# Turned tiles first in their step, and a last half tile in quarters, in a fused attention and mLSTM block

## Chip, core and metric

One core of a Trainium2 chip (trn2) runs the whole block. The metric is the device time of one execution in microseconds, lower is better. "Low parts" below are the remainders of numbers split in two: every float32 matrix is used as a high part (rounded to the TensorE input format) and a low part (what the rounding lost), and a product of two matrices is made of three matmuls, high x high, high x low and low x high.

## What is computed

For 512 tokens of width 1024: an RMS norm, one projection to ten groups of columns, attention with 8 heads of 64 on rotated queries and keys, an mLSTM with 4 heads of 128, both normed and gated, one output projection, an RMS norm of it, and the residual. At this length all blocks are selected, so that attention is plain causal attention. The part that the change works on is the end of it:

```python
ya = rms_norm(attention(...), attn_out_g[l]) * jax.nn.silu(az)
ym = jax.nn.sigmoid(mo) * hm * jax.nn.silu(mz)
y = jnp.einsum('bsc,cd->bsd', jnp.concatenate([ya, ym], axis=-1), w_out[l])
x = x + rms_norm(y, post_norm_g[l])
```

## The kernel before

Tokens lie in 4 tiles of 128 partitions. Weights come in slots of 256 KB through a ring; ScalarE cuts the high part (`cut`, L708), VectorE or GpSimd the low part (L922, L591). A first stage runs slot by slot: projections, and beside them the mLSTM heads, with the keys and queries turned by TensorE (`turn_k`, L1539, and `turn_q`, L1549) and split by `kt_high` (ScalarE, L696) and `kt_low` (VectorE, L1132). `qk_low` (L1052) is the low part of the mLSTM's queries and keys, which `head_scores` needs.

The second stage is a list of steps, 0 to 39, written out by hand in `EVENTS`; each engine walks the same list in program order and meets the others at semaphores. Step s holds, for a unit of attention (one head of one query tile, 32 in all, tile 3 first):

- even s: TensorE makes the scores of units s and s+1 (`pair_scores`, L1646), into banks 6 and 7; VectorE masks them (L1256); ScalarE makes the exponential (`exp_of`, L854);
- TensorE transposes the probabilities of unit s-2 (L1696), ScalarE copies their high part (`pt_high`, L862), VectorE makes the low part (`pt_low`, L1262);
- TensorE multiplies unit s-3 with the values (`wide_values`, L1667, for tiles 3 to 1, `tile_values`, L1679, for tile 0). For odd s VectorE sums two finished units (`y2_sum`, L1247) out of bank 2. `wide_values` of an even unit waits for the sum of the two units before it, since it writes the same bank.

In between TensorE works at products of the projections and of the output (`z_part`, `om`, `oa`, L1355 to L1357), two to four in a step. In eight steps (9, 13, 17, 21, 23, 25, 31, 36; `TURNS`) a finished tile of ym or ya is turned so that it can be multiplied with the output weights: TensorE transposes it into bank 6 (`turn`, L1615), ScalarE copies it (`turn_high`, L801), VectorE makes the low part (`turn`, L1213). The next `pair_scores` waits for that, because bank 6 is the same one.

The output is made in halves of 512 columns for each of 4 tiles, as `(i, c)` with i = 0 to 3 and c = 0, 1; i = 3 is the first tile of tokens. The steps of a half are: four products (`oa`), the sum with the mLSTM's part (`y_sum`, L1292), its squares (ScalarE, L899), the product with the norm's gain (`y_gain` on GpSimd, L640; for i = 3 on VectorE, L1298); for each tile the mean (`y_mean`, L1302 and L1304), the reciprocal root (GpSimd, L556), the write (`y_out`, L1312) and the stores (`store`, all on the SP queue, L458).

Of the kernel before, what the change touches and what calls it, by code (L numbers as in the profile page):

```python
# [20 lines left out]
ALU = mybir.AluOpType  # L21
ACT = mybir.ActivationFunctionType

P = 128
# [67 lines left out]
for _h, _g in enumerate(("az", "ak", "av", "aq")):  # L92
# [18 lines left out]
N_WIDE = AH * (NT - 1)  # L111
EVENTS = {}

PRIORITY = ("mz", "mz_late", "z", "om_out", "cut", "slot", "z_part", "om", "oa", "q_T", "q_out", "ya_half", "y", "ya", "y_sq", "ya_sq",
            "ya_ms", "y_fin", "y_end", "turn")


def _event(step, kind, *what):
# [34 lines left out]
OA_ORDER = ((0, 0, 27), (1, 0, 28), (0, 1, 30), (1, 1, 33), (2, 0, 35), (2, 1, 36), (3, 0, 37), (3, 1, 38))  # L153
OA_OF = {(_i, _c): _n for _n, (_i, _c, _at) in enumerate(OA_ORDER)}
for _i, _c, _at in OA_ORDER:
    for _k in range(4):
        _event(_at, "oa", _i, 4 * _c + _k)
    _event(_at + int(_at < 35), "y", _i, _c)
    _event(_at + 1, "y_sq", _i, _c)
for _i, (_mean, _end) in enumerate(((33, 34), (35, 36), (37, 37), (39, 39))):  # L160
    _event(_mean, "y_fin", _i)
    _event(_end, "y_end", _i)
for _i in range(NT):
    _s = AH * _i + AH - 1 + LAG_PV
    _late = int(_i < NT - 1)
# [9 lines left out]
def _sharers():  # L175

    where, last, now = {}, {0: ("mz", 0), 1: ("mz", 1)}, 1
    starts = {"z_part": "z", "om": "om", "oa": "oa"}  # L180
    for s in range(STEPS):
        for kind, what in [e for e in EVENTS.get(s, ()) if e[0] in starts]:
            if what[-1] % (NK if kind == "z_part" else 4) == 0:
                user = (starts[kind], OA_OF[what[0], what[1] // 4] if kind == "oa" else what[0])
                if user == ("oa", OA_OF[NT - 1, 0]):
# [15 lines left out]
def build(nc, x, pre_g, w_in, i_bias, f_bias, conv_w, conv_b, attn_g, mlstm_g, w_out, post_g, rope, out):  # L201
    with ExitStack() as ctx:
# [57 lines left out]
        msa = sb("msa", [P, NT])  # L260
        ra = sb("ra", [P, NT])
        ssy = sb("ssy", [P, 2 * NT])
        msy = sb("msy", [P, NT])
        ry = sb("ry", [P, NT])

# [33 lines left out]
        ya = f_part(F_YA, 2, AW)  # L299
        yb = f_part(F_Y, 2, D)  # L300
        yg = tmp.rearrange("p a c -> p (a c)")
        kT_hi = r_part(R_KT, 4, SEQ)
        kT_lo = r_part(R_KT + 4 * SEQ, 4, SEQ)
        v_hl = r_part(R_V, NT * AH, 2 * DH)
# [115 lines left out]
        oa_ps = sem("oa_ps")  # L420
        y_done = sem("y_done")
        ssy_done = sem("ssy_done")
        msy_done = sem("msy_done")
        ry_done = sem("ry_done")
        y_gained = sem("y_gained")
# [35 lines left out]
        def _(sp):  # L461
# [45 lines left out]
            sp.wait_ge(out_done[0], 32)  # L507
            load_residual(3)
            store(sp, 2)
            store(sp, 3)  # L510
            for i in range(NT):
                sp.wait_ge(out_done[i], 32)


        @block.gpsimd
        def _(g):
# [118 lines left out]
            def y_gain(i, c):  # L635

                n = OA_OF[i, c]
                g.wait_ge(post_in, 16)
                g.wait_ge(ssy_done, n + 1)
                g.tensor_tensor(yb[:, i % 2, c * AW:(c + 1) * AW], yb[:, i % 2, c * AW:(c + 1) * AW],  # L640
                                post[:, c * AW:(c + 1) * AW], ALU.mult).then_inc(y_gained, 1)

            for s in range(STEPS):
                for kind, what in EVENTS.get(s, ()):
                    i = what[0]
                    if kind == "cut":
                        cut(i)
                    elif kind == "ya" and i < NT - 2:
                        ya_norm(i)
                    elif kind == "ya_ms":  # L650
                        g.wait_ge(msa_done, i + 1)
                        rsqrt(ra[:, i:i + 1], msa[:, i:i + 1]).then_inc(ra_done, 1)
                    elif kind == "y_sq" and i < NT - 1:
# [46 lines left out]
        def _(a):  # L700
# [163 lines left out]
            for s in range(STEPS):  # L864
                events = EVENTS.get(s, ())
                for kind, what in events:
                    if kind == "mz":
                        mz_evac(a, *what)
                    elif kind == "z":
                        z_evac(a, *what)  # L870
                    elif kind == "om_out":
                        om_evac(a, *what)
                    elif kind == "cut":
                        cut(*what)
                if LAG_T <= s < NU + LAG_T:
# [1 line left out]
                if s < NU:  # L877
                    exp_of(s)
                for kind, what in events:
                    if kind == "turn":  # L880
                        turn_high(*what)
                    elif kind == "mz_late":
                        mz_evac(a, *what)
                for kind, what in events:
                    i = what[0]
                    if kind == "q_out":
                        q_high(i)
                    elif kind == "ya_sq":
                        a.wait_ge(ya_done, i + 1)
                        junk_free()  # L890
                        squares["ya"] += 1
                        a.activation(gains[:], ya[:, i % 2, :], ACT.Square,
                                     accum_out=ssa[:, i:i + 1]).then_inc(ssa_done, 1)
                    elif kind == "y_sq":
                        i, c = what
                        a.wait_ge(y_done, OA_OF[i, c] + 1)
                        junk_free()
                        squares["y"] += 1
                        a.activation(gains[:], yb[:, i % 2, c * AW:(c + 1) * AW], ACT.Square,  # L899
                                     accum_out=ssy[:, 2 * i + c:2 * i + c + 1]).then_inc(ssy_done, 1)  # L900

        @block.vector
        def _(v):
# [255 lines left out]
            for b in range(S_QK, LAST_SLOT + 1):  # L1161
# [123 lines left out]
            def y_sum(i, c):  # L1285
# [4 lines left out]
                if i >= 2:  # L1290
                    v.wait_ge(out_ready, 2 * (i - 1))
                v.scalar_tensor_tensor(out=yb[:, i % 2, cols], in0=shared("oa", n)[:], scalar=ra[:, i:i + 1],  # L1292
                                       in1=y_mlstm[:, c, NT - 1 - i, :], op0=ALU.mult, op1=ALU.add).then_inc(y_done, 1)
                if i == NT - 1:
                    v.wait_ge(y_done, n + 1)
                    v.wait_ge(post_in, 16)
                    v.wait_ge(ym_gated, NT)
                    v.tensor_tensor(yg[:, cols], yb[:, i % 2, cols], post[:, cols], ALU.mult).then_inc(y_gained, 1)  # L1298

            def y_mean(i):  # L1300
# [5 lines left out]
            def y_out(i):  # L1306
                v.wait_ge(ry_done, i + 1)
                v.wait_ge(xr_in[i], 16)
                v.wait_ge(y_gained, OA_OF[i, 1] + 1)
                for c in range(2):  # L1310
                    cols = slice(c * AW, (c + 1) * AW)
# [4 lines left out]
            for s in range(STEPS):  # L1316
                events = EVENTS.get(s, ())
                if s < NU:
                    mask(s)
                if 0 <= s - LAG_FOLD < N_WIDE and s % 2 == 1:  # L1320
                    y2_sum(s - LAG_FOLD)
                for kind, what in events:
# [4 lines left out]
                if LAG_T <= s < NU + LAG_T:  # L1327
                    pt_low(s - LAG_T)
                for kind, what in events:
                    if kind == "turn":  # L1330
                        turn(*what)
                    elif kind == "mz_late":
                        mz_gate(*what)
                for kind, what in events:
                    if kind == "q_out":
# [6 lines left out]
                        ya_scale(*what)  # L1342
                    elif kind == "y":
                        y_sum(*what)
                    elif kind == "y_fin":
                        y_mean(*what)
                    elif kind == "y_end":
                        y_out(*what)
# [3 lines left out]
        def _(pe):  # L1352
# [265 lines left out]
            def oa(i, k):  # L1618
# [8 lines left out]
                if kk == 3:  # L1627
                    mm.then_inc(oa_ps, 1)

            def pair_scores(s):  # L1630

                t, h = unit(s)
# [50 lines left out]
            for s in range(STEPS):  # L1683
                events = EVENTS.get(s, ())
                if s < NU and s % 2 == 0:
                    pair_scores(s)
                u = s - LAG_T
                if 0 <= u < NU:
                    t, h = unit(u)
# [10 lines left out]
                    turn_y2(s - LAG_YT)  # L1700
                    turn_y2(s - LAG_YT + 1)
                for kind, what in events:
                    if kind == "turn":
                        turn(*what)
                for kind, what in events:
                    if kind == "slot":
                        mz_slot(*what)
                    elif kind == "q_T":
# [4 lines left out]
                        om_part(*what)  # L1713
                    elif kind == "oa":
                        oa(*what)
                u = s - LAG_PV
                if 0 <= u < NU:
                    pe.wait_ge(pt_lo, u + 1)
# [32 lines left out]
```

## Time and profile before

| | us |
|---|---|
| median of 3 runs | 335.34 (334.81 to 335.36) |
| profiled execution | 335.24 |
| its span | 333.5 |
| TensorE busy | 317.8 |
| VectorE busy | 227.5 |
| ScalarE busy | 172.2 |
| GpSimd busy | 99.9 |

The span is what the profiler records of the instructions; 1.7 us lie around it. Matmuls are pipelined, so that a single one of 512 columns is shown as 0.39 us long while the next one starts 0.23 us later: distances between starts say more than durations. The mean granted TensorE clock is 0.992 of full speed. The engines' steps run one behind the other within each engine, and an idle time in front of an instruction is put down to the semaphore that came last.

### The profile page before, as it was taken

How to read it: one execution, taken by the hardware profiler on the slowest of the kernel's cores; microseconds unless marked ns; L12 is line 12 of the kernel's file. 1: busy time of each engine (PE TensorE's matmuls, PEld its weight loads, DVE VectorE, ACT ScalarE, POOL GpSimd, SP SyncE). 2: the span in 40 equal slices, each digit the busy share in tenths (PEclk: the TensorE clock that was granted, in tenths of full speed). 3: DMA queues.
4: the chain of work that ended last, by engine and by line, in shares of the span. 5: the costliest groups of instructions: out<-in, count | busy, mean ns of one | idle time of the engine just before them, and what ended most of it. 6: DMA issues, size and time to landing. Idle time of an engine off the chain costs nothing.

```text
span 333.5 us, 5022 instructions
## 1 busy us (share of the span) xinstructions
PE 317.8 (95%) x1614; PEld 260.9 (78%) x1614; DVE 227.5 (68%) x530; ACT 172.2 (52%) x341; POOL 99.9 (30%) x121
## 2 busy tenths in 40 slices
PE   8999999999999999899999999999999998998790
PEld 5887788888888888688888888788888887887580
DVE  2544999678996589876995487575766743435785
ACT  3448653696373524845346522655548647354330
POOL 8001003207240240002400054880025724154451
PEclk9999999999999999999999999999999999999996
DMA  7931544842736552246425232200001401602044
GB/s 225 286 96 32 166 129 107 164 140 82 127 85 157 147 87 64 63 126 132 76 63 159 70 89 66 90 37 2 0 2 63 172 19 43 211 23 105 0 156 160
DMA packets 26873, 33.51 MB, mean 100 GB/s; under 512 B 3752, under 2 KB 15056, under 8 KB 26848
## 3 DMA queue, kind: packets, MB, share of 16 engines
q1 hardware_dynamic: 25712, 30.51, 30.6%
q0 software_dynamic: 1120, 2.68, 6.2%
q8 instruction: 13, 0.21, 0.3%
q14 instruction: 12, 0.10, 0.1%
q10 hardware_dynamic: 16, 0.00, 0.0%
HBM read 31.06 MB, written 2.13 MB: 100 GB/s over the span
## 4 chain that ended last, share of the span: by engine, by line
PE 84%; DVE 9%; issue 4%; ACT 2%; DVEq 0%; POOLq 0%; POOL 0%; ACTq 0%
PE bank L1355 21%; PE bank L1357 21%; PE bank L1356 21%; PE bank L1402 3%; PE bank L1646 3%; PE bank L1696 3%; PE bank L1667 2%; PE bank L1490 1%; PE bank L1383 1%; PE bank L1370 1%; DVE farena L1043 1%; DVE xT_lo L1213 1%; PE bank L1657 1%; ACT xT_hi L801 1%; DVE w_lo L922 1%
## 5 line engine op out<-in xcount | busy, mean ns | idle before, releaser
L1355 PE MATMUL bank<-w_hi,xT_hi 128*128 128x512 f32 x272 | 110.7, 407 | 0.0
L1357 PE MATMUL bank<-w_hi,xT_lo 128*128 128x512 f32 x272 | 106.7, 392 | 0.0
L1356 PE MATMUL bank<-w_lo,xT_hi 128*128 128x512 f32 x272 | 106.1, 390 | 0.0
L708 ACT ACTIVATE w_hi<-w_raw 128x512 fp32r<-128x512 f32 x88 | 53.2, 626 | 59.2 <-PE bank L1357 58.8
L1357 PEld LDWEIGHTS bank<-w_hi,xT_lo 128*128 128x128 f32 x272 | 51.0, 188 | 11.4
L1355 PEld LDWEIGHTS bank<-w_hi,xT_hi 128*128 128x128 f32 x272 | 51.2, 188 | 9.1 <-issue 0.4
L1356 PEld LDWEIGHTS bank<-w_lo,xT_hi 128*128 128x128 f32 x272 | 51.3, 189 | 8.8
L922 DVE TENSOR_TENSOR w_lo<-w_raw,w_hi 128x512 fp32r<-128x512 f32 x64 | 45.1, 719 | 5.0 <-ACT w_hi L708 4.5
L591 POOL TENSOR_TENSOR w_lo<-w_raw,w_hi 128x512 fp32r<-128x512 f32 x24 | 31.2, 1320 | 48.4 <-ACT w_hi L708 48.4
L862 ACT ACTIVATE rarena<-bank 128x512 fp32r<-128x512 f32 (+3 forms) x32 | 13.8, 435 | 26.0 <-PE bank L1696 26.0
L1256 DVE CUSTOM_DVE_ANT_0 farena<-bank,causal 128x512 f32<-128x512 f32 (+3 forms) x32 | 15.4, 483 | 17.1 <-PE bank L1646 17.1
L1355 PE MATMUL bank<-xT_hi,w_hi 128*128 128x512 f32 x64 | 25.7, 402 | 0.0
L1357 PE MATMUL bank<-xT_hi,w_lo 128*128 128x512 f32 x64 | 25.1, 393 | 0.0
L1356 PE MATMUL bank<-xT_lo,w_hi 128*128 128x512 f32 x64 | 25.0, 391 | 0.0
L1262 DVE TENSOR_TENSOR rarena<-bank,rarena 128x512 fp32r<-128x512 f32 (+3 forms) x32 | 15.6, 489 | 13.7 <-ACT rarena L862 13.5
L1043 DVE SCALAR_TENSOR_TENSOR farena<-farena,pcol 128x512 f32<-128x512 f32 x24 | 18.8, 783 | 0.8
L854 ACT ACTIVATE farena<-farena,mx 128x512 f32<-128x512 f32 (+3 forms) x32 | 17.8, 556 | 2.6 <-DVE mx L1256 2.5
L571 POOL DMA_DIRECT2D farena<-g_rows x16 | 8.6, 546 | 33.8 <-DVE farena L1063 32.2
L1063 DVE SCALAR_TENSOR_TENSOR farena<-bank,farena 128x512 f32<-128x512 f32 (+3 forms) x16 | 7.8, 488 | 14.4 <-PE bank L1357 14.4
L556 POOL TENSOR_TENSOR vr<-vs,mhalf 128x2 f32<-128x2 f32 x8 | 5.7, 709 | 37.5 <-DVE vs L1102 37.5
L1696 PE MATMUL bank<-ident,farena 128*128 128x128 f32 x80 | 14.9, 284 | 0.0
L1646 PE MATMUL bank<-rarena 64*128 64x512 f32 (+3 forms) x96 | 11.7, 347 | 3.2 <-DVE xT_lo L1213 1.9
(195 smaller groups left out, 522.8 us busy)
## 6 DMA issues: line engine op xcount, KB each, us to landing
w_raw<-in_w_in SPq DMA_DIRECT2D x72, 256.0 KB, 2.9
w_raw<-in_w_out SPq DMA_DIRECT2D x16, 256.0 KB, 2.7
farena<-in_x SPq DMA_DIRECT2D x4, 256.0 KB, 4.7
farena<-in_x SPq DMA_DIRECT2D x2, 512.0 KB, 7.5
farena<-g_rows POOLq DMA_DIRECT2D x4, 256.0 KB, 3.9
silu_az<-in_x SPq DMA_DIRECT2D x2, 512.0 KB, 3.7
w_raw<-in_x SPq DMA_DIRECT2D x2, 512.0 KB, 3.3
out_y<-silu_az SPq DMA_DIRECT2D x4, 256.0 KB, 2.0
```

What stands on the lines that cost most here:

```text
L591: g.tensor_tensor(w_lo[:, n % RING, :], w_raw[:, n % RAW, :], w_hi[:, n % RING, :].bitcast(F32), ALU.subtract).then_inc(w_lo_done[n % 2], 1)
L708: a.activation(w_hi[:, n % RING, :], w_raw[:, n % RAW, :], ACT.Copy).then_inc(w_hi_done, 1)
L854: a.activation(prob[:, s % 2, 0:n], sm[:, s % 2, 0:n], ACT.Exp, scale=-1.0, bias=mx[:, s:s + 1], accum_out=rsum[:, s:s + 1]).then_inc(prob ...
L922: v.tensor_tensor(w_lo[:, n % RING, :], w_raw[:, n % RAW, :], f32(w_hi[:, n % RING, :]), ALU.subtract).then_inc(w_lo_done[n % 2], 1)
L1043: ins = v.scalar_tensor_tensor(out=acc, in0=u[:, j:j + SEQ], scalar=tap[j], in1=acc, op0=ALU.mult, op1=ALU.add)
L1256: v.tensor_tensor_reduce(sm[:, s % 2, 0:n], bank[6 + s % 2][:, 0:n], causal[:, SEQ - n:], -Q_SCALE, BIG, ALU.add, ALU.min, mx[:, s:s + 1]) ...
L1262: v.tensor_tensor(pT[:, 2 * (u % 2) + 1, 0:n], bank[4 + u % 2][:, 0:n], f32(pT[:, 2 * (u % 2), 0:n]), ALU.subtract).then_inc(pt_lo, 1)
L1355: pe.matmul(o, hi, m_hi, start=start, stop=False)
L1356: pe.matmul(o, hi, m_lo, start=False, stop=False)
L1357: return pe.matmul(o, lo, m_hi, start=False, stop=stop)
L1646: mm = pe.matmul(bank[6 + q][:, 0:n], lhs, keys_of[half, h // 2, 0:n], start=step == 0, stop=step == 2)
L1696: mm = pe.transpose(bank[4 + u % 2][:, j * P:(j + 1) * P], prob[:, u % 2, j * P:(j + 1) * P], ident[:])
```

## The change

The three engines take a turned tile first in its step: TensorE before it transposes probabilities, ScalarE before it copies the transposed probabilities and makes the exponential (but after the weight cuts of the step), VectorE right after the mask, ahead of `y2_sum` and `pt_low`.

The half (3, 1) is made as two quarters of 256 columns, each with its own sum, gain and squares; quarter 1 goes to bank 7. The sum y(3, 0) moves from step 37 to 38, behind the mean of tile 2; its gain moves from VectorE to GpSimd. In step 37 GpSimd makes the root of tile 2 before the gain of (2, 1), no longer after it. The write of the half (2, 0) stands in step 38, that of (2, 1) in step 41, behind the last mean. The mean of tile 3 is prepared with one quarter's squares and finished with the other's by one operation. The last stores are (3, 0) and the last quarter from SP, the third quarter from ScalarE's queue.

`kt_low(0)` and `kt_low(1)` stand behind the cut of one block earlier each.

```diff
 for _i, _c, _at in OA_ORDER:
+    if (_i, _c) == (NT - 1, 1):
+        for _q in range(2):
+            for _k in range(4):
+                _event(_at, "oa_q", _q, _k)
+            _event(_at + 1 + _q, "y_q", _q)
+            _event(_at + 1 + _q, "y_q_sq", _q)
+        continue
     for _k in range(4):
         _event(_at, "oa", _i, 4 * _c + _k)
-    _event(_at + int(_at < 35), "y", _i, _c)
+    _late = int(_at < 35 or _i == NT - 1)
+    _event(_at + _late, "y", _i, _c)
     _event(_at + 1, "y_sq", _i, _c)
-for _i, (_mean, _end) in enumerate(((33, 34), (35, 36), (37, 37), (39, 39))):
+for _i, (_mean, _end) in enumerate(((33, (34, 34)), (35, (36, 36)), (37, (38, 41)), (41, (41, 41)))):
     _event(_mean, "y_fin", _i)
-    _event(_end, "y_end", _i)
+    for _c in range(2):
+        _event(_end[_c], "y_end", _i, _c)
...
# SP
-            store(sp, 3)
+            sp.wait_ge(out_ready, 2 * NT - 1)
+            sp.dma_start(out[0, 0:P, 0:AW], xr[NT - 1][:, 0:AW]).then_inc(out_done[NT - 1], 16)
+            sp.wait_ge(out_ready, 2 * NT + 1)
+            sp.dma_start(out[0, 0:P, quarter[1]], xr[NT - 1][:, quarter[1]]).then_inc(out_done[NT - 1], 16)
...
# GpSimd
-                    elif kind == "y_sq" and i < NT - 1:
+                    elif kind == "y_sq":
                         y_gain(*what)
...
# ScalarE
                         om_evac(a, *what)
+                for kind, what in events:
+                    if kind == "turn":
+                        turn_high(*what)
                     elif kind == "cut":
                         cut(*what)
                 if LAG_T <= s < NU + LAG_T:
...
-                    if kind == "turn":
-                        turn_high(*what)
-                    elif kind == "mz_late":
+                    if kind == "mz_late":
                         mz_evac(a, *what)
...
+            a.wait_ge(out_ready, 2 * NT)
+            a.dma_start(out[0, 0:P, quarter[0]], xr[NT - 1][:, quarter[0]]).then_inc(out_done[NT - 1], 16)
...
# VectorE
-                if KT_AT + 2 <= b < KT_AT + 2 + NT:
+                if KT_AT + 4 <= b < KT_AT + 2 + NT:
                     kt_low(b - KT_AT - 2)
...
                 cut(b + AHEAD)
+                if KT_AT + 1 <= b < KT_AT + 3:
+                    kt_low(b - KT_AT - 1)
...
+            def y_quarter(q):
+                i, cols = NT - 1, quarter[q]
+                v.wait_ge(oaq_ps, q + 1)
+                if q == 0:
+                    v.wait_ge(ra_done, NT)
+                src = shared("oa", OA_OF[i, 1])[:, 0:AW // 2] if q == 0 else bank[7][:, 0:AW // 2]
+                v.scalar_tensor_tensor(out=yb[:, i % 2, cols], in0=src, scalar=ra[:, i:i + 1],
+                                       in1=y_mlstm[:, 1, 0, q * (AW // 2):(q + 1) * (AW // 2)], op0=ALU.mult,
+                                       op1=ALU.add).then_inc(yq_done, 1)
+                v.wait_ge(yq_done, q + 1)
+                v.wait_ge(post_in, 16)
+                v.wait_ge(ym_gated, NT)
+                v.tensor_tensor(yg[:, cols], yb[:, i % 2, cols], post[:, cols], ALU.mult).then_inc(yq_gained, 1)
...
                 if s < NU:
                     mask(s)
+                for kind, what in events:
+                    if kind == "turn":
+                        turn(*what)
                 if 0 <= s - LAG_FOLD < N_WIDE and s % 2 == 1:
                     y2_sum(s - LAG_FOLD)
...
# TensorE
                 if s < NU and s % 2 == 0:
                     pair_scores(s)
+                for kind, what in events:
+                    if kind == "turn":
+                        turn(*what)
                 u = s - LAG_T
                 if 0 <= u < NU:
```

## Rows read from the trace of the kernel before

**Rows 1.** Page, first part: busy time, share of the span and instructions.

```profile
PE 317.8 (95%) x1614; PEld 260.9 (78%) x1614; DVE 227.5 (68%) x530; ACT 172.2 (52%) x341; POOL 99.9 (30%) x121
```

**Rows 2.** Timeline of step 9: start, duration, engine, line, operation, output<-input.

```profile
235.96 0.60 PE L1696 MATMUL bank<-ident,farena 128*128 128x128 f32 x4
236.38 0.69 DVE L1247 TENSOR_REDUCE num<-bank 128x256 f32<-128x512 f32 x1
236.60 0.60 ACT L862 ACTIVATE rarena<-bank 128x512 fp32r<-128x512 f32 x1 [1.34 <-PE bank L1696]
...
237.69 0.59 ACT L801 ACTIVATE xT_hi<-bank 128x512 fp32r<-128x512 f32 x1
238.22 0.64 PE L1667 MATMUL bank<-rarena 128*128 128x256 f32 x4
238.31 0.69 DVE L1213 TENSOR_TENSOR xT_lo<-bank,xT_hi 128x512 fp32r<-128x512 f32 x1 [0.39 <-ACT xT_hi L801]
239.15 0.79 PE L1646 MATMUL bank<-rarena 64*128 64x384 f32 x6 [0.29 <-DVE xT_lo L1213]
```

**Rows 3.** Waits (total us, times, longest), then timeline of turns 1 and 4.

```profile
PE bank L1646 <- DVE xT_lo L1213: 1.9, 4, 0.9
...
247.55 0.49 PE L1696 MATMUL bank<-ident,farena 128*128 128x128 f32 x3
250.52 0.80 PE L1646 MATMUL bank<-rarena 64*128 64x384 f32 x6 [0.30 <-DVE xT_lo L1213]
...
280.81 0.37 ACT L862 ACTIVATE rarena<-bank 128x256 fp32r<-128x256 f32 x1
283.02 0.55 PE L1646 MATMUL bank<-rarena 64*128 64x128 f32 x6 [0.93 <-DVE xT_lo L1213]
```

**Rows 4.** Timeline of TensorE's values in steps 32 to 34.

```profile
307.95 0.44 PE L1679 MATMUL bank<-rarena 128*128 128x128 f32 x2
...
312.56 0.69 PE L1679 MATMUL bank<-rarena 128*128 128x128 f32 x4 [1.26 <-DVE rarena L1262]
```

**Rows 5.** Timeline around the second key tile and the head scores.

```profile
139.60 0.69 DVE L1132 TENSOR_TENSOR rarena<-bank,rarena 128x512 fp32r<-128x512 f32 x1 [0.88 <-ACT rarena L696]
...
140.89 0.39 PE L1355 MATMUL bank<-rarena 128*128 128x512 f32 x1
```

**Rows 6.** Timeline of the end; a group by form (busy, mean ns); a DMA issue.

```profile
323.14 0.75 DVE L1292 SCALAR_TENSOR_TENSOR farena<-bank,ra,gy 128x512 f32<-128x512 f32 x1 [0.59 <-PE bank L1357]
325.44 0.39 PE L1357 MATMUL bank<-w_hi,xT_lo 128*128 128x512 f32 x1
326.92 0.75 DVE L1292 SCALAR_TENSOR_TENSOR farena<-bank,ra,gy 128x512 f32<-128x512 f32 x1
328.93 0.54 POOL L556 TENSOR_TENSOR ry<-msy,mhalf 128x1 f32<-128x1 f32 x1 [3.38 <-DVE msy L1304]
329.51 1.41 DVE L1312 SCALAR_TENSOR_TENSOR silu_az<-stage,ry,silu_az 128x512 f32<-128x512 f32 x2 [0.66 <-POOL ry L556]
...
L1063 DVE SCALAR_TENSOR_TENSOR farena<-bank,farena 128x256 f32<-128x256 f32 x4 | 1.7, 424 | 5.3 <-PE bank L1357 5.3
...
out_y<-silu_az SPq DMA_DIRECT2D x4, 256.0 KB, 2.0
```

**Rows 7.** Timeline: VectorE and GpSimd at once, on operands in SBUF.

```profile
300.62 0.75 DVE L1275 TENSOR_TENSOR farena<-farena,rrec 128x512 f32<-128x512 f32 x1
300.79 1.72 POOL L640 TENSOR_TENSOR farena<-farena,stage 128x512 f32<-128x512 f32 x1
...
320.02 1.30 POOL L640 TENSOR_TENSOR farena<-farena,stage 128x512 f32<-128x512 f32 x1
320.42 0.75 DVE L1292 SCALAR_TENSOR_TENSOR farena<-bank,ra,gy 128x512 f32<-128x512 f32 x1 [0.40 <-PE bank L1357]
...
321.15 1.41 DVE L1312 SCALAR_TENSOR_TENSOR w_raw<-farena,ry,w_raw 128x512 f32<-128x512 f32 x2
321.31 0.98 POOL L556 TENSOR_TENSOR ra<-msa,mhalf 128x1 f32<-128x1 f32 x1
```

More of the change, by code:

```diff
@@ L112 @@
 EVENTS = {}
-PRIORITY = ("mz", "mz_late", "z", "om_out", "cut", "slot", "z_part", "om", "oa", "q_T", "q_out", "ya_half", "y", "ya", "y_sq", "ya_sq",
-            "ya_ms", "y_fin", "y_end", "turn")
+PRIORITY = ("mz", "mz_late", "z", "om_out", "cut", "slot", "z_part", "om", "oa", "oa_q", "q_T", "q_out", "ya_half", "y", "y_q", "ya",
+            "y_fin", "y_sq", "y_q_sq", "ya_sq", "ya_ms", "y_end", "turn")
 def _event(step, kind, *what):
@@ L179, in _sharers @@
     where, last, now = {}, {0: ("mz", 0), 1: ("mz", 1)}, 1
-    starts = {"z_part": "z", "om": "om", "oa": "oa"}
+    starts = {"z_part": "z", "om": "om", "oa": "oa", "oa_q": "oa"}
     for s in range(STEPS):
         for kind, what in [e for e in EVENTS.get(s, ()) if e[0] in starts]:
-            if what[-1] % (NK if kind == "z_part" else 4) == 0:
+            if kind == "oa_q" and what[0] == 0 and what[1] == 0:
+                user = ("oa", OA_OF[NT - 1, 1])
+            elif kind != "oa_q" and what[-1] % (NK if kind == "z_part" else 4) == 0:
                 user = (starts[kind], OA_OF[what[0], what[1] // 4] if kind == "oa" else what[0])
+            else:
+                user = None
+            if user:
                 if user == ("oa", OA_OF[NT - 1, 0]):
@@ L262, in build @@
         ssy = sb("ssy", [P, 2 * NT])
+        ssq = sb("ssq", [P, 2])
         msy = sb("msy", [P, NT])
@@ L301, in build @@
         yg = tmp.rearrange("p a c -> p (a c)")
+        quarter = [slice(AW, AW + AW // 2), slice(AW + AW // 2, D)]
         kT_hi = r_part(R_KT, 4, SEQ)
@@ L422, in build @@
         ssy_done = sem("ssy_done")
+        oaq_ps = sem("oaq_ps")
+        yq_done = sem("yq_done")
+        ssq_done = sem("ssq_done")
+        yq_gained = sem("yq_gained")
         msy_done = sem("msy_done")
@@ L509, in _ @@
             store(sp, 2)
-            store(sp, 3)
+            sp.wait_ge(out_ready, 2 * NT - 1)
+            sp.dma_start(out[0, 0:P, 0:AW], xr[NT - 1][:, 0:AW]).then_inc(out_done[NT - 1], 16)
+            sp.wait_ge(out_ready, 2 * NT + 1)
+            sp.dma_start(out[0, 0:P, quarter[1]], xr[NT - 1][:, quarter[1]]).then_inc(out_done[NT - 1], 16)
             for i in range(NT):
-                sp.wait_ge(out_done[i], 32)
+                sp.wait_ge(out_done[i], 32 + 16 * (i == NT - 1))
         @block.gpsimd
@@ L639, in y_gain @@
                 g.wait_ge(ssy_done, n + 1)
-                g.tensor_tensor(yb[:, i % 2, c * AW:(c + 1) * AW], yb[:, i % 2, c * AW:(c + 1) * AW],
-                                post[:, c * AW:(c + 1) * AW], ALU.mult).then_inc(y_gained, 1)
+                if i == NT - 1:
+                    g.wait_ge(ym_gated, NT)
+                g.tensor_tensor((yg if i == NT - 1 else yb[:, i % 2])[:, c * AW:(c + 1) * AW],
+                                yb[:, i % 2, c * AW:(c + 1) * AW], post[:, c * AW:(c + 1) * AW],
+                                ALU.mult).then_inc(y_gained, 1)
             for s in range(STEPS):
@@ L900, in _ @@
                                      accum_out=ssy[:, 2 * i + c:2 * i + c + 1]).then_inc(ssy_done, 1)
+                    elif kind == "y_q_sq":
+                        q = what[0]
+                        a.wait_ge(yq_done, q + 1)
+                        junk_free()
+                        if q:
+                            a.wait_ge(ssq_done, q)
+                        a.activation(gains[:, 0:AW // 2], yb[:, (NT - 1) % 2, quarter[q]], ACT.Square,
+                                     accum_out=ssq[:, q:q + 1]).then_inc(ssq_done, 1)
+            a.wait_ge(out_ready, 2 * NT)
+            a.dma_start(out[0, 0:P, quarter[0]], xr[NT - 1][:, quarter[0]]).then_inc(out_done[NT - 1], 16)
         @block.vector
@@ L1293, in y_sum, with y_mean @@
                                        in1=y_mlstm[:, c, NT - 1 - i, :], op0=ALU.mult, op1=ALU.add).then_inc(y_done, 1)
-                if i == NT - 1:
[L1295 to L1300, printed above, removed]
+            def y_quarter(q):
[11 more added lines that the diff above has]
+                v.tensor_tensor(yg[:, cols], yb[:, i % 2, cols], post[:, cols], ALU.mult).then_inc(yq_gained, 1)
+                if q == 1:
+                    v.wait_ge(ssy_done, 2 * NT - 1)
+                    v.wait_ge(ssq_done, 1)
+                    link(v.tensor_scalar(msy[:, i:i + 1], ssy[:, 2 * i:2 * i + 1], ssq[:, 0:1], 1.0 / D, ALU.add,
+                                         ALU.mult))
+                    link(v.tensor_scalar(msy[:, i:i + 1], msy[:, i:i + 1], EPS, None, ALU.add))
+            def y_mean(i):
+                if i == NT - 1:
+                    v.wait_ge(ssq_done, 2)
+                    v.scalar_tensor_tensor(out=msy[:, i:i + 1], in0=ssq[:, 1:2], scalar=1.0 / D, in1=msy[:, i:i + 1],
+                                           op0=ALU.mult, op1=ALU.add).then_inc(msy_done, 1)
+                    return
                 v.wait_ge(ssy_done, OA_OF[i, 1] + 1)
@@ L1304, in y_mean, with y_out @@
                 v.tensor_scalar(msy[:, i:i + 1], msy[:, i:i + 1], EPS, None, ALU.add).then_inc(msy_done, 1)
-            def y_out(i):
+            def y_out(i, c):
+                cols = slice(c * AW, (c + 1) * AW)
                 v.wait_ge(ry_done, i + 1)
                 v.wait_ge(xr_in[i], 16)
-                v.wait_ge(y_gained, OA_OF[i, 1] + 1)
-                for c in range(2):
-                    cols = slice(c * AW, (c + 1) * AW)
+                if i == NT - 1:
+                    v.wait_ge(y_gained, OA_OF[i, 0] + 1)
+                    v.wait_ge(yq_gained, 2)
+                else:
+                    v.wait_ge(y_gained, OA_OF[i, c] + 1)
+                for cols in quarter if (i, c) == (NT - 1, 1) else (cols,):
                     v.scalar_tensor_tensor(out=xr[i][:, cols], in0=(yg if i == NT - 1 else yb[:, i % 2])[:, cols],
@@ L1329, in _ @@
                 for kind, what in events:
-                    if kind == "turn":
-                        turn(*what)
-                    elif kind == "mz_late":
+                    if kind == "mz_late":
                         mz_gate(*what)
@@ L1344, in _ @@
                         y_sum(*what)
+                    elif kind == "y_q":
+                        y_quarter(*what)
                     elif kind == "y_fin":
@@ L1628, in oa, with oa_quarter @@
                     mm.then_inc(oa_ps, 1)
+            def oa_quarter(q, kk):
+                o = shared("oa", OA_OF[NT - 1, 1])[:, 0:AW // 2] if q == 0 else bank[7][:, 0:AW // 2]
+                low_done(pe, S_OA + 4 + kk)
+                if kk == 0 and q == 0:
+                    shared_free("oa", OA_OF[NT - 1, 1])
+                elif kk == 0:
+                    pe.wait_ge(masked, NU)
+                mm = product(o, *x_part(4 + kk, 0), *w_part(S_OA + 4 + kk, slice(q * (AW // 2), (q + 1) * (AW // 2))),
+                             kk == 0, kk == 3)
+                if kk == 3:
+                    mm.then_inc(oaq_ps, 1)
             def pair_scores(s):
@@ L1702, in _ @@
                 for kind, what in events:
-                    if kind == "turn":
-                        turn(*what)
-                for kind, what in events:
                     if kind == "slot":
@@ L1715, in _ @@
                         oa(*what)
+                    elif kind == "oa_q":
+                        oa_quarter(*what)
                 u = s - LAG_PV
```

## Prediction

> **What bounds the kernel now.** Read the page first: TensorE is busy for 95% of the span, the other engines for 30 to 68% [rows 1]. So a change pays only where TensorE sits idle, or behind its last product. The waits of TensorE show one repeated idle place in the attention steps: the pair of scores (L1646) waits for the low half of a turned tile (L1213), four times, 1.9 us in all [rows 3]. The timeline of step 9 shows what stands in front of it [rows 2]: transposes at 235.96, ScalarE copies pT (236.60), does an exp, and only then copies the turned tile (237.69); VectorE subtracts (238.31, 0.69 us), and the scores start at 239.15. TensorE's last four products before (L1667, 238.22; four in 0.64 us with the last one's full length, so 0.117 us apart) are through at 238.69. So the real gap is 0.46 us, and the 0.29 of the wait column is less only because the ends of matmuls are modelled. The same reading gives 0.47, 0.55 and 0.99 us for turns 1, 2 and 4, together 2.47 us. Turns 3 and 5 have no gap: their steps hold three or four products of 3 x 0.23 us each instead of two.
>
> The second place is the end [rows 6]. The last matmul starts at 325.44, yet the sum that reads it (L1292) starts at 326.92, because VectorE is still writing another tile (L1312). After it come gain, mean, the reciprocal root on GpSimd (328.93), two writes of 1.41 us (329.51 to 330.92), and a store that lands 2.0 us after issue. All of that is exposed.
>
> **Turned tiles first in their step.** TensorE, ScalarE and VectorE all take the turn ahead of their other work. The scores then no longer wait for pT's copy and exp. But on VectorE the turn also passes the sum y2 (L1247), and TensorE's values of the same odd step (L1667) overwrite the bank that y2 reads: wide_values waits for y2_done. Before, y2 ran at 236.38, in VectorE's idle time, far ahead of 238.22 [rows 2]. Now it is queued behind a subtraction that itself waits for ScalarE. I rebuild the path with the distances of the rows, from the first transpose: 0.64 to ScalarE's copy (235.96 to 236.60), 0.62 to VectorE's subtraction (237.69 to 238.31), 0.61 to y2 (one such operation to the next), 0.69 for y2, 0.15 from VectorE's end to TensorE's start (239.00 to 239.15), 0.47 for the four products: scores 3.18 us behind the first transpose. Before they came 3.19 us behind it. The stall moves from the scores to the values and keeps its size.
> - Turn 0: 0.0 us.
> - Turn 1 has three products (0.35 us): 0.64 + 0.62 + 0.61 + 0.84 + 0.35 = 3.06, against 250.52 - 247.55 = 2.97 [rows 3]: +0.1. Turn 2, a step of the same shape where ScalarE is also still cutting weights: +0.1.
> - Turn 4: four weight cuts stay ahead of the turn on ScalarE, which comes free at 280.81 [rows 3]. 280.81 + 0.62 + 0.61 + 0.84 + 0.33 = 283.21 against 283.02: +0.2.
> - Turns 3 and 5: the path to y2 is 2.56 us long and 0.15 more to TensorE, TensorE's own work there 2.7 and more: 0. That cover is thin at turn 3; were it gone, some 0.1 us.
> - Turn 6 (step 31) has no y2. Here the turn passes pT of unit 29, whose low part comes about 1.2 us later, so values(29) (307.95) and the 12 products behind it slip by about 1.3 us. What covers this is TensorE's idle 1.26 us before 312.56 [rows 4], which ends with the copy of pT of unit 30 behind y(0,1), and VectorE reaches y(0,1) about when it did: -0.1 to +0.2, taken as 0.
> Sum of this part +0.4 us. Bounds: -2.3 if y2 did not hold the values (all gaps but 0.2 us of turn 4 gone), +0.7 with a slower restart of 0.07 us after each stall.
>
> **Key low parts.** kt_low(0) was already the instruction right behind that cut (nothing else stands between the two places in that block), so it doesn't move. Only kt_low(1) moves, ahead of the low part qk_low(5) (L1052). But kt_low(1) waits for ScalarE until 139.60 [rows 5], in either order. VectorE then stands still with qk_low(5) and a cut queued behind it; qk_low(5) ends at about 139.60 + 0.60 + 0.68 = 140.88. The scores that need it start at 140.89 and would start 0.15 later: 141.03. +0.1 us; the cut is one of six ahead and costs nothing. Bounds 0 and +0.2.
>
> **The last half tile in quarters.** 24 matmuls of 256 columns at 0.117 us [rows 2] are 2.8 us for 2.73 before, +0.1 on TensorE and not exposed as long as VectorE comes later. On VectorE a 256-column operation takes 0.42 (L1063) to 0.48 us, against 0.75 for 512 [rows 6]; a product of two SBUF tensors 0.42. The gain is the later mean of tile 2's second write, no second gain on VectorE for the first half, and short last links. The danger is that the two engines hold each other up. In the rows of before, a VectorE operation with two SBUF inputs (L1275, 300.62) waited for GpSimd, and GpSimd's next product (L640, 300.79, 1.72 us instead of 1.30) waited for it and ended 1.14 us behind it; the small root L556 at 321.31, 0.54 us when alone, took 0.98 beside a write L1312 and ended 0.4 behind the first one [rows 6, 7]. A sum out of PSUM beside GpSimd's product kept its 0.75 us (320.42), so only operations with both inputs in SBUF are meant [rows 7].
>
> The Trainium skill says the same as a rule (SBUF — State Buffer, section "Who interferes with whom"): a VectorE instruction with two SBUF inputs and a GpSimd instruction that reads SBUF exclude each other, and whoever issues first holds the port for the whole instruction. The rows agree, and the rule speaks against this change, which puts GpSimd's product of the half (3,0) beside VectorE's quarters; with it the end is as worked out below, without it 1.2 us sooner.
>
> The end, in the clock of before: writes of tile 1 end at 322.56 [rows 7]; mean of tile 2, root on GpSimd 322.96 to 323.50, then y_gain(2,1) 323.47 to 324.76. VectorE: y(3,0) 323.14 to 323.89 [rows 6]; write (2,0) dispatched 323.81, held, ends 325.36 (0.6 behind GpSimd). GpSimd: y_gain(3,0) ends 325.36 + 1.15 = 326.51. VectorE: sum of quarter 0 until 325.76, its gain held until 326.79, sum of quarter 1 326.71 to 327.19 (its products were ready at 325.95), gain to 327.65, three small steps of the mean 0.24 apart, the last at 328.05. Then VectorE dispatches the deferred write (2,1) at 328.15, 0.1 us before GpSimd's root can start, and the root ends 0.40 behind it, at 329.30, as the row at 321.31 did. Last writes: 329.34, then 0.67, 0.40 and 0.48 on: end 330.89, against 330.92. The last store is 128 KB instead of 256: between 0 and 0.35 us sooner in landing, taken as 0.15. Together -0.2 us.
>
> **Sum**: 335.24 (span 333.5 and 1.7 around it) + 0.4 + 0.1 - 0.2 = 335.5. The median of the runs is 0.1 above the profiled one, so 335.6.
>
> **Rivals.**
> 1. *The end pays.* If VectorE and GpSimd don't hold each other up there, quarter 0 is through by 325.54, quarter 1's sum starts with its products at 325.95, root 327.52 to 328.06, end 329.68: -1.24, with the store -1.4. Total 335.24 + 0.5 - 1.4 + 0.1 = 334.4. For it: the small offsets (0.34 us between GpSimd's gain and VectorE's write, 0.1 between write and root) could fall the other way; against it: the rows above. 0.18. Half of it (only the root escapes, 0.46 us) would be 335.1.
> 2. *Turns pay*, y2 finds room: -2.3 instead of +0.4, 332.9. For it: the wait rows name L1213 alone; against it: program order, in which y2 stands behind the turn and values behind y2. 0.10.
> 3. *Slower.* At 324.76 GpSimd's next product goes ahead of the waiting write (2,0). It then ends at 326.05, the write at 326.65, the quarters follow at 326.57 and 327.42, root 330.0, end 331.6: 0.7 later than in the forecast, 336.3. It decides at one point, who goes first when both wait. Against it: at 300.79 GpSimd had just ended one product, and the waiting L1275 went first. 0.17, with the slips of turns 3, 4 and 6 in it, which reach 336.1 together.
> 4. *The change doesn't do what it says*: that is the forecast itself for turns and keys, stalls that keep their size under another name.
>
> **Chances.** Forecast 335.6 (its own range 335.2 to 336.0) 0.55, rival 1 0.18, rival 2 0.10, rival 3 0.17. A difference under 0.2% (0.67 us: 334.67 to 336.01) can't be told from none. Faster takes rivals 1 and 2, less the half case of rival 1: 0.25. Slower takes rival 3 and a little of the forecast's edge: 0.20. Same 0.55. The range leaves out rival 2 and the edge of rival 3: 334.3 to 336.3.
>
> **What would show it.** In the trace after: waits of L1646 for L1213 gone, and new ones of L1667's for y2 (L1247) of 0.4 to 1.2 us at turns 0, 1, 2 and 4, with pairs of scores not sooner behind the step's first transpose; kt_low(1) still behind ScalarE's copy, the head scores 0.1 later; the gain of quarter 0 over 0.9 us long, and the last root near 1.0 us. Wrong, if the scores come 2.7 us behind the first transpose of step 9, or if the sum of quarter 1 starts within 0.4 us of its last product.

## The result and the profile after

The changed kernel takes 336.23 us (median of 5 runs, 336.15 to 336.78), the kernel before beside it 335.0 (334.77 to 335.36): ratio 1.004, 95% interval 1.0025 to 1.0054. It is 1.2 us slower. The profiled execution took 336.23 with a span of 334.3. The profiled execution of before (335.24) was one of its slower ones, and by 137 us it was 0.2 to 0.5 us behind most of the other traces, so I compare distances within a trace, not clock times across two.

The waits of TensorE in the changed kernel (total, times, longest; L1745 is `wide_values`, L1286 is `y2_sum`, L1724 is `pair_scores`):

```profile
PE bank L1745 <- DVE num L1286: 2.2, 4, 1.0
PE bank L1435 <- DVE xT_lo L970: 1.5, 1, 1.5
PE bank L1724 <- issue: 1.3, 1, 1.3
PE bank L1757 <- DVE rarena L1301: 1.2, 1, 1.2
```

The four waits of the scores for the turned tile [rows 3] are gone. Four waits of the values for y2 stand in their place. The timeline of step 9 shows how (L1680 turn, L827 and L1252 its high and low part):

```profile
235.95 0.60 PE L1680 MATMUL bank<-ident,gy 128*128 128x128 f32 x4
236.58 0.60 ACT L827 ACTIVATE xT_hi<-bank 128x512 fp32r<-128x512 f32 x1 [1.33 <-PE bank L1680]
237.21 0.69 DVE L1252 TENSOR_TENSOR xT_lo<-bank,xT_hi 128x512 fp32r<-128x512 f32 x1 [0.76 <-ACT xT_hi L827]
237.82 0.68 DVE L1286 TENSOR_REDUCE num<-bank 128x256 f32<-128x512 f32 x1
238.65 0.71 PE L1745 MATMUL bank<-rarena 128*128 128x256 f32 x4 [0.28 <-DVE num L1286]
239.29 0.79 PE L1724 MATMUL bank<-rarena 64*128 64x384 f32 x6
```

The turned tile is ready 1.1 us sooner (L1252 starts at 237.21, before it was 238.31 [rows 2]), and y2 starts at 237.82 where it was 236.38. VectorE idled 0.76 us in front of the turn's low part with y2 queued behind it. The scores come 3.34 us behind the step's first transpose, before 3.19.

The end of the changed kernel, VectorE and GpSimd (L1331 and L1339 sums, L1345 gain of a quarter, L665 gain on GpSimd, L1374 writes, L579 root):

```profile
324.04 0.75 DVE L1331 SCALAR_TENSOR_TENSOR farena<-bank,ra,gy 128x512 f32<-128x512 f32 x1 [0.29 <-PE bank L1422]
324.33 1.29 POOL L665 TENSOR_TENSOR farena<-farena,stage 128x512 f32<-128x512 f32 x1
324.71 1.46 DVE L1374 SCALAR_TENSOR_TENSOR w_raw<-farena,ry,w_raw 128x512 f32<-128x512 f32 x1
...
325.68 1.63 POOL L665 TENSOR_TENSOR stage<-farena,stage 128x512 f32<-128x512 f32 x1
326.09 0.47 DVE L1339 SCALAR_TENSOR_TENSOR farena<-bank,ra,gy 128x256 f32<-128x256 f32 x1
...
326.60 1.00 DVE L1345 TENSOR_TENSOR stage<-farena,stage 128x256 f32<-128x256 f32 x1
...
327.52 0.47 DVE L1339 SCALAR_TENSOR_TENSOR farena<-bank,ra,gy 128x256 f32<-128x256 f32 x1
...
328.02 0.42 DVE L1345 TENSOR_TENSOR stage<-farena,stage 128x256 f32<-128x256 f32 x1
...
328.90 0.75 DVE L1374 SCALAR_TENSOR_TENSOR w_raw<-farena,ry,w_raw 128x512 f32<-128x512 f32 x1
329.04 1.02 POOL L579 TENSOR_TENSOR ry<-msy,mhalf 128x1 f32<-128x1 f32 x1 [1.72 <-DVE msy L1356]
330.09 1.54 DVE L1374 SCALAR_TENSOR_TENSOR silu_az<-stage,ry,silu_az 128x512 f32<-128x512 f32 x3 [0.44 <-POOL ry L579]
```

Three operations are longer than their like: the write (2,0) 1.46 us for the 0.75 of the write (2,1) at 328.90, the gain of quarter 0 1.00 for the 0.42 of quarter 1's at 328.02, the root 1.02 for 0.54 [rows 6]. From the transposes of turn 7 to the last write it is 13.76 us (317.87 to 331.63), before 13.95 (316.97 to 330.92). The stores land no sooner for being smaller:

```profile
out_y<-silu_az SPq DMA_DIRECT2D x3, 256.0 KB, 2.1
out_y<-silu_az ACTq DMA_DIRECT2D x1, 128.0 KB, 2.1
```

### The profile page after: what moved, and what is told of

It reads as the page before. It is cut to its first block, busy times and chain, and to the rows that moved or that the text cites. A ratio compares the mean times of both kernels' runs of the same rounds, so it can differ in the third digit from the quotient of the medians.

```text
span 334.3 us, 5061 instructions
## 1 busy us (share of the span) xinstructions
PE 318.7 (95%) x1626; PEld 260.9 (78%) x1626; DVE 227.3 (68%) x533; ACT 172.6 (52%) x343; POOL 101.5 (30%) x122
## 4 chain that ended last, share of the span: by engine, by line
PE 82%; DVE 8%; issue 4%; ACT 2%; POOL 1%; DMA 1%; DVEq 0%; POOLq 0%; ACTq 0%
PE bank L1420 21%; PE bank L1422 20%; PE bank L1421 20%; PE bank L1467 3%; PE bank L1724 3%; PE bank L1777 3%; PE bank L1745 3%; PE bank L1555 1%; PE bank L1448 1%; PE bank L1435 1%; DVE farena L1080 1%; PE bank L1680 1%; ACT xT_hi L827 1%; DVE num L1286 1%; DMA w_raw<-in_w_out 1%
## 5 line engine op out<-in xcount | busy, mean ns | idle before, releaser
L1420 PE MATMUL bank<-w_hi,xT_hi 128*128 128x512 f32 (+1 forms) x276 | 111.3, 403 | 0.0
L1422 PE MATMUL bank<-w_hi,xT_lo 128*128 128x512 f32 (+1 forms) x276 | 107.4, 389 | 0.0
L1421 PE MATMUL bank<-w_lo,xT_hi 128*128 128x512 f32 (+1 forms) x276 | 106.8, 387 | 0.0
L1422 PEld LDWEIGHTS bank<-w_hi,xT_lo 128*128 128x128 f32 x276 | 51.8, 188 | 11.1
L1420 PEld LDWEIGHTS bank<-w_hi,xT_hi 128*128 128x128 f32 x276 | 52.0, 189 | 9.0 <-issue 0.4
L1421 PEld LDWEIGHTS bank<-w_lo,xT_hi 128*128 128x128 f32 x276 | 52.1, 189 | 8.7
L579 POOL TENSOR_TENSOR vr<-vs,mhalf 128x2 f32<-128x2 f32 x8 | 5.7, 708 | 37.2 <-DVE vs L1139 37.2
L1745 PEld LDWEIGHTS bank<-rarena 128*128 128x128 f32 x72 | 11.5, 188 | 5.6 <-issue 4.0
L1252 DVE TENSOR_TENSOR xT_lo<-bank,xT_hi 128x512 fp32r<-128x512 f32 x8 | 5.5, 690 | 14.4 <-ACT xT_hi L827 14.4
```

Of the source, the lines that this page charges most:

```text
L1420: pe.matmul(o, hi, m_hi, start=start, stop=False)
L1421: pe.matmul(o, hi, m_lo, start=False, stop=False)
L1422: return pe.matmul(o, lo, m_hi, start=False, stop=stop)
L1745: mm = pe.matmul(bank[2][:, 2 * P * (u % 2):2 * P * (u % 2 + 1)], v_hl[:, j * AH + h, :], pT[:, 2 * (u % 2):2 * (u % 2) + 2, j * P:(j + 1) ...
```

## The experiments

Theory A: the loss is y2 queued behind the turn on VectorE. Rival B: the loss is in the end. Everything is timed beside the kernel before (334.9 us).

**The turns alone.** The three moves of the turn on top of the kernel before.

> Only the turned tiles first in their step, on all three engines; end and keys as before. Theory A (y2 is queued behind the turn on VectorE and the values of the same step wait for it, four times, with a slow restart of about 0.2 us each): the pairs of scores behind turns 0, 1, 2 and 4 come 0.2 to 0.3 us later each, 1.0 us slower in all, about 336.0 where the kernel before has 335.0. Rival B (the end is what costs): no difference here, 335.0. What the edit was to bring if y2 did not hold the values: 332.8.

336.0 us, ratio 1.0029 (1.0018 to 1.0039), and the same four waits:

```profile
PE bank L1669 <- DVE num L1248: 2.2, 4, 1.0
```

The turns alone lose 1.1 us. B falls as the only cause.

**The end alone.** All edits but the turns' and the keys'.

> Only the end: quarters, later write, gain of (3,0) on GpSimd, three last stores on two queues. Theory A: last write 0.2 us sooner behind the last turn, the last store 0.1 later to the end of the span, so 334.9, within 0.2 us of before, unless time outside the span is added. Rival B: 1.0 or more slower, 336.0. If the end pays as meant: 333.8.

335.01 us, ratio 1.0005 (0.9996 to 1.0014): no difference that can be told. B falls; rival 1 of the prediction (the end pays) falls too.

**The keys alone.**

```diff
-                if KT_AT + 2 <= b < KT_AT + 2 + NT:
+                if KT_AT + 4 <= b < KT_AT + 2 + NT:
                     kt_low(b - KT_AT - 2)
...
                 cut(b + AHEAD)
+                if KT_AT + 1 <= b < KT_AT + 3:
+                    kt_low(b - KT_AT - 1)
```

> Only kt_low(1) ahead of qk_low(5). By the trace of the changed kernel, where step 3 of the attention stage starts at the same time as before: 0.0, 335.0. By the recorded working: +0.1. The rival that keys carry the loss: 336.

335.44 us, ratio 1.0013 (1.0004 to 1.0022): a little slower, against my later reading of 0.0 and with the recorded one. The timeline shows kt_low(1) (L1132) waiting for ScalarE longer than before, qk_low(5) (L1052) behind it, and the head scores (the product on rarena) behind that:

```profile
139.21 0.69 DVE L1132 TENSOR_TENSOR rarena<-bank,rarena 128x512 fp32r<-128x512 f32 x1 [1.49 <-ACT rarena L696]
139.82 0.68 DVE L1052 TENSOR_TENSOR rarena<-farena,rarena 128x512 fp32r<-128x512 f32 x1
140.55 0.50 PE L1357 MATMUL bank<-rarena 128*128 128x512 f32 x1
140.89 0.40 PE L1358 MATMUL bank<-rarena 128*128 128x512 f32 x1
```

From the third key tile's transposes to the fourth's it is 4.09 us here (137.27 to 141.36), 4.08 in the changed kernel, and 3.90 to 3.93 in the kernel before and in the variants without the edit: +0.17 us. The larger part of it lies inside the head scores: their second product starts 0.34 us behind the first, 0.23 in the kernel before (140.89 to 141.12). What more there is in the 0.5 us between the medians is not explained; the interval begins at 0.1.

**y2 first.** The turns as in the first experiment, but on VectorE:

```diff
                 if s < NU:
                     mask(s)
-                for kind, what in events:
-                    if kind == "turn":
-                        turn(*what)
                 if 0 <= s - LAG_FOLD < N_WIDE and s % 2 == 1:
                     y2_sum(s - LAG_FOLD)
+                for kind, what in events:
+                    if kind == "turn":
+                        turn(*what)
```

> As the turns alone, but VectorE makes y2 ahead of the turn's low part; TensorE and ScalarE take the turn first. Theory A: y2 runs at its old time, the values do not wait, and the scores follow at once: the four gaps of 0.46, 0.47, 0.55 and 0.99 us go except 0.2 us of the last, 2.2 us faster, 332.8. Rival (the stall of the values has another cause, such as the order of TensorE's own transposes): stays at 336.

332.83 us, ratio 0.9938 (0.9925 to 0.995). One instruction's place on one engine is worth 3.2 us against the turns alone, and the sign of the edit with it. Step 9:

```profile
235.94 0.69 DVE L1248 TENSOR_REDUCE num<-bank 128x256 f32<-128x512 f32 x1
...
236.15 0.60 ACT L801 ACTIVATE xT_hi<-bank 128x512 fp32r<-128x512 f32 x1 [1.33 <-PE bank L1617]
...
236.78 0.69 DVE L1214 TENSOR_TENSOR xT_lo<-bank,xT_hi 128x512 fp32r<-128x512 f32 x1 [0.16 <-ACT xT_hi L801]
...
237.78 0.63 PE L1669 MATMUL bank<-rarena 128*128 128x256 f32 x4
...
238.34 0.80 PE L1648 MATMUL bank<-rarena 64*128 64x384 f32 x6
```

y2 fills the time in which VectorE waits for ScalarE, the turn's low part still starts as soon as the copy lets it (0.63 us behind it, as in the changed kernel), and values and scores follow without a wait, 2.83 us behind the first transpose at 235.51. The four values take 0.56 us to the scores here (237.78 to 238.34); behind their wait in the changed kernel the same four take 0.64 (238.65 to 239.29). The kernel before, too, has 0.56 in flow where scores follow, and 0.47 where transposes follow (at 235.96 [rows 2]):

```profile
232.09 0.63 PE L1667 MATMUL bank<-rarena 128*128 128x256 f32 x4
232.65 0.80 PE L1646 MATMUL bank<-rarena 64*128 64x384 f32 x6
...
235.49 0.64 PE L1667 MATMUL bank<-rarena 128*128 128x256 f32 x4
```

**The changed kernel with y2 first.** The same edit on the changed kernel.

> The changed kernel with one edit: VectorE makes y2 ahead of the turn's low part. Theory A (its only loss in the middle is y2 behind the turn): 336.2 - 1.0 - 2.1 = 333.1. If the changed end interacts with it, more than 0.3 us off that.

332.95 us, ratio 0.9938 (0.9923 to 0.9953). The one order explains the loss of the middle; end and keys add little on top.

**The end, without GpSimd's gain of (3,0).** The end alone, and the half (3,0) written without the norm's gain (code shortened: the write of this half also reads the sum itself and waits for it):

```diff
-                    elif kind == "y_sq":
+                    elif kind == "y_sq" and what[0] < NT - 1:
                         y_gain(*what)
```

> The end alone (as e2_tail), with GpSimd's product with the norm's gain of the half (3,0) left out of the computation, so that this half is written without that gain. Theory A (GpSimd's product holds the product of quarter 0 for 0.6 us, and with it quarter 1's sum, which is late): the product of quarter 0 takes 0.42 us instead of 0.99, the write (2,0) still 1.45, the root still 1.0; quarter 1's sum starts with its products, 0.6 us sooner, 334.4. Rival (TensorE's products set the start of quarter 1's sum): no change, 335.0.

334.55 us, ratio 0.9994 (0.9982 to 1.0007). The time is where it was expected, though alone it can't be told from no change; the rows can:

```profile
325.55 0.42 DVE L1342 TENSOR_TENSOR stage<-farena,stage 128x256 f32<-128x256 f32 x1
...
325.90 0.48 DVE L1336 SCALAR_TENSOR_TENSOR farena<-bank,ra,gy 128x256 f32<-128x256 f32 x1
```

The gain of quarter 0 takes 0.42 us for 0.99 in the end alone, and the sum of quarter 1 starts 2.92 us behind the sum y(3,0) (322.98) for 3.47. The root is still 1.02 us.

**The late write last.** The end alone, with the write (2,1) and its store behind the last quarter (the event at step 42 for 41).

> The end alone (as e2_tail), with the late write (2,1) moved behind the last quarter. Theory A (the late write holds the last root for 0.48 us): the root takes 0.54 us instead of 1.02, the last quarter is written 0.5 us sooner, and the late write then ends 0.2 us later than the last quarter did, so 335.2 in all. Rival (the root is long for another reason): the root stays at 1.0 us, 335.7.

335.05 us, ratio 1.0006 (0.9997 to 1.0015).

```profile
327.71 0.54 POOL L582 TENSOR_TENSOR ry<-msy,mhalf 128x1 f32<-128x1 f32 x1 [1.72 <-DVE msy L1356]
328.29 1.55 DVE L1374 SCALAR_TENSOR_TENSOR silu_az<-stage,ry,silu_az 128x512 f32<-128x512 f32 x3 [0.66 <-POOL ry L582]
```

The root is 0.54 us when no write stands beside it. The late write then costs its 0.7 us at the very end, so nothing is won: using the wait for the root gives back 0.48 of 0.7.

**GpSimd's earlier gains held back.** If the two engines hold each other up at the end, they do so elsewhere too. In the kernel before, VectorE's gating of ya takes more than twice the 0.69 us that it takes alone, both times while GpSimd's gain runs (300.79 to 302.51 [rows 7] for the first one):

```profile
301.41 1.65 DVE L1279 TENSOR_TENSOR silu_az<-farena,silu_az 128x512 f32<-128x512 f32 x1
315.25 1.67 DVE L1279 TENSOR_TENSOR silu_az<-farena,silu_az 128x512 f32<-128x512 f32 x1
```

On top of y2 first:

```diff
                 g.wait_ge(ssy_done, n + 1)
+                if (i, c) == (0, 0):
+                    g.wait_ge(ya_gated, NT - 1)
+                if (i, c) == (1, 1):
+                    g.wait_ge(out_ready, 2)
```

> The turns with y2 first (as e4_y2_first, 332.8), and GpSimd's gain of (0,0) waits for ya of tile 2, its gain of (1,1) for the write of tile 0. Theory A extended: in the kernel before VectorE's gating of ya (1.65 us, twice, 0.69 alone) is held by GpSimd's gains and stands on the path to TensorE's idle 1.3 us before step 30 and 0.9 us before turn 7. Both shorten to 0.7 us, 0.96 us each, 330.9. Rival (something else ends those two idle times): 332.8.

330.84 us, ratio 0.9878 (0.9863 to 0.9892). Both gatings are short, and GpSimd's gain starts behind them:

```profile
299.30 0.69 DVE L1284 TENSOR_TENSOR silu_az<-farena,silu_az 128x512 f32<-128x512 f32 x1
...
300.16 1.28 POOL L644 TENSOR_TENSOR farena<-farena,stage 128x512 f32<-128x512 f32 x1 [1.45 <-DVE silu_az L1284]
...
312.16 0.69 DVE L1284 TENSOR_TENSOR silu_az<-farena,silu_az 128x512 f32<-128x512 f32 x1
```

TensorE's wait before the scores of step 30, 1.3 us in the kernel before, the changed one and y2 first, is 0.4 us here:

```profile
PE bank L1652 <- issue: 0.4, 1, 0.4
```

The wait of 0.9 us before turn 7 is shorter too: from the scores of step 30 to turn 7's transposes it is 12.61 us here, 13.55 in y2 first. Adding two waits to an engine that is 30% busy took 2.0 us off, half of it at each of the two places.

**The end with less holding.** The changed kernel with y2 first and the old place of the keys; the gain of (3,0) on VectorE behind its sum, GpSimd's gain of (2,1) ahead of the root.

> The changed end and turns with y2 first, keys as before; the gain of (3,0) back on VectorE behind its sum, and GpSimd's gain of (2,1) ahead of the root again. Theory A: quarter 1's sum starts 0.3 to 0.6 us sooner than in e2_tail, the root is still held by the late write; 332.5. Rival (holding is not what costs in the end): 332.9 as the sum of e4_y2_first and e2_tail.

332.43 us, ratio 0.9925 (0.991 to 0.994): 0.4 us below y2 first with the old end. The two intervals overlap, but the traces agree with it: from turn 7's transposes to the end of the span it is 15.86 us, 16.52 in y2 first and 16.41 in the end alone. The write (2,0) and the gain of quarter 0 take 0.75 and 0.43 us, the sum of quarter 1 starts 0.5 us sooner behind y(3,0) than in the end alone (2.92 for 3.47 us), the root is still 1.02.

**Together.** The last two: GpSimd's earlier gains held back, and the end with less holding.

> The edits of e7_held and e8_tailT together: turns with y2 first, GpSimd's gains of (0,0) and (1,1) held back, changed end with the gain of (3,0) on VectorE. Theory A: they stand at different places of the path and add up, 330.84 - 0.4 = 330.4. Rival: the earlier turn 7 lets the end meet GpSimd's later gain, and nothing is added, 330.8.

330.34 us, ratio 0.9865 (0.9848 to 0.9881). The two add up.

**Turn ahead of the cuts.** On top of it, ScalarE copies the turned tile ahead of the weight cuts of its step.

> As e9_best, with ScalarE's copy of the turned tile ahead of the weight cuts of its step too. Theory A: the last 0.2 us wait of the scores behind turn 4 goes, and nothing waits for the cuts: 0.2 us faster than e9_best, 330.2. Rival (the cuts, 0.6 us later, come late for the output's products through GpSimd): 330.4 or slower.

330.22 us, ratio 0.9861 (0.9846 to 0.9876). The last wait of the scores for a turned tile (0.2 us) is gone from the waits, and from the scores of step 22 to those of step 24 it is 7.80 us for 8.03; in the times the expected 0.2 is within the scatter. This is the fastest of all, 6.0 us below the changed kernel and 4.7 below the kernel before.

## Why the prediction was wrong

The forecast was 335.6, no difference; measured is 336.23, slower by 0.4%. The time lies in the range, the side was wrong: +0.3 us was forecast for the change, +1.2 measured. The mechanism was right at each place, and the sizes were off. By the steps of the prediction:

- *The stall moves from the scores to the values*: shown, in the waits after, by the turns alone, and from the other side by y2 first. Rival 2 (turns pay) falls for this change. Its price with y2 out of the way, 2.3 us, was right within 0.2: 2.1 measured in the times, 1.95 in the distances between the scores.
- *Sum of the turns +0.4 us*: this is the term that failed; it measured +1.0. The distances from one pair of scores to the next in the two traces give +0.15, +0.26, +0.28 and +0.24 for turns 0, 1, 2 and 4, where the prediction had 0, 0.1, 0.1 and 0.2, and +0.04 for turn 3. Two things were priced too low, of about equal weight. The first is the last link, from the values to the scores. The prediction took it from the spacing of the values among themselves, 0.47 us for four. That holds when transposes follow, but when scores follow it is 0.56 even in flow (the rows under y2 first). That is 0.09 us in each of turns 0, 1 and 2, 0.3 in all; for turn 4 the 0.33 was right. The second is the restart: behind a wait the values take 0.64 us to the scores instead of 0.56, that is 0.08 more, four times, 0.3 in all. The prediction named a restart of 0.07 as a bound, which was right, but put it at 0 in the sum. With both, its own sums give +0.16, +0.26, +0.27 and +0.26. One figure is less sure than it looks: turn 2's distance is 5.94 us in the trace of before, but 6.04 to 6.07 in the four variants that also have the old order of the turns, so its +0.28 may be 0.15 and the sum about 0.85.
- *The gaps of before, 2.47 us in all*: the same last link makes them 0.1 us too long at turns 0, 1 and 2; they are 0.36, 0.37, 0.45 and 1.00, 2.2 in all. y2 first takes 0.37, 0.37, 0.45 and 0.76 off these distances, just these gaps less what is left at turn 4.
- *Turn 6 at 0*: right. Values(29) start at 310.12 behind a wait of 1.19 us, and values(30) follow at 313.46, 0.90 us later than in the trace of before, like the scores of step 30 ahead of them (0.96); the way from the scores of step 30 to turn 7 is 13.55 us, before 13.61.
- *Keys +0.1*: 0.17 in the trace, 0.1 to 0.7 by the interval.
- *The end -0.2*: counted from the sum y(3,0), the schedule written out ahead was 0.1 us late at the write (2,0) and the gain of quarter 0, and 0.16 late at the last write (7.75 us for 7.59); the three holdings came where it had them. From turn 7 to the last write it was 0.19 shorter, where 0.03 was forecast. The store's 0.15 was wrong: 128 KB land in 2.1 us, 256 KB in 2.0. The end as a whole gives +0.1 in the times of the end alone (-0.1 to +0.5 by the interval) and -0.1 in the traces.
- *Rival 3* (GpSimd goes ahead of a waiting write) did not happen: at 325.68 GpSimd's next gain waits for the write (2,0), as at 300.79 in the kernel before. The slower side, with a chance of 0.20 in all, came from the term that I had thought settled.

In sum 1.0 + 0.17 + 0.1 = 1.3 us, 1.1 with the end at -0.1; measured 1.2. That the time still came within the stated range is due to its width; the forecast itself, no difference, was wrong.

What the prediction leaned on for the end is what the Trainium skill states (SBUF — State Buffer, section "Who interferes with whom"): a VectorE instruction with two SBUF inputs and a GpSimd instruction that reads SBUF exclude each other for a whole instruction. The runs agree, from both sides: 0.99 to 0.42 us with GpSimd's product left out, 1.02 to 0.54 with the write moved, 1.65 to 0.69 with GpSimd held back.

The Trainium skill (DMA: Bandwidth & Descriptors, section "Anatomy of one DMA — SWDGE (gpsimd) path") gives, for GpSimd's path, a fixed part of about 2.0 us and a part by size; by it the smaller store would land about 0.3 us sooner (an estimate from that page). The stores here go by SP's and ScalarE's queues, so they don't test it; on these queues the trace shows no such gain, 2.1 us for 128 KB and 2.0 for 256 KB.

## What to carry to other kernels

When a step is moved to the front on an engine that runs in order, list what it is now ahead of, and for each who waits for it; here one sum that reads a bank decided between 1.1 us lost and 2.1 us won. A wait that disappears under one name can come back under another of the same size: look for the total idle time of the engine that bounds, not for the name. An operation whose duration is double that of its like is a finding: here two products of GpSimd, which is 30% busy, held 2 us of the critical path. And price a step by the distance to the very instruction that follows it, not by the spacing inside the step: that alone hid 0.3 us here.

## What was not expected of the hardware

- A wait of TensorE in front of the values (weights of 128 x 128, 256 columns) costs 0.08 us more than the wait itself: four take 0.64 us to the scores behind one, 0.56 in flow. The scores, with weights of 64 rows, show no such surcharge: 0.72 us to the next transposes behind a wait (239.15 to 239.87) and in flow (232.65 to 233.37). Why the two differ is open; it wasn't tried apart.
- Values followed by scores take 0.09 us longer to the next instruction than values followed by transposes (0.56 for 0.47 us). The reason is open too.
- Between back-to-back products on GpSimd a waiting VectorE operation came first (the write at 324.71 ahead of the gain at 325.68; in the kernel before, the one at 300.62 ahead of the gain at 300.79). In both its record starts ahead of GpSimd's, so that the rows don't tell whether VectorE has precedence or whoever came first.
- A store of 128 KB from SP or ScalarE's queue landed no sooner than one of 256 KB (2.1 us).
